# mLSTM keys and queries of 1024 tokens from seven block products of sums in place of eight; key turns moved by threes behind gate units

## The reference, cut to what matters

```
p = h @ w_in                       # h: 2176 x 1024; q, k, v, o, g of 8 heads x 128, and 32 gates
for each head:                     # forward and backward direction
    states C, n from k * wk and v, chunk by chunk
    num = (q k^T * w) v + w0 * q C ;  den likewise ;  hm = num / den
y = ((hf + hb) * sigmoid(o) * silu(g)) @ w_out
x = x + gate * y ; final RMSNorm
```

## Time and profile before

| | |
|---|---|
| time, median of 3 runs | 2608.09 us (2607.71 to 2608.79) |
| span of the profiled execution | 2606.4 us, for which the page gives no time but this |
| busy share of the span | PE 98%, PEld 86%, DVE 49%, ACT 36%, POOL 25% |
| mLSTM heads | seven periods of 150.0 us, and the last head, which ends near 2414 us |
| DMA | 223.84 MB, mean 86 GB/s |

### The profile page before, as it was taken

One profiled execution on the slowest core, in us unless ns is written; L12 is line 12 of the kernel. 1 busy time (PEld: TensorE's weight loads), 2 busy tenths in 40 slices (PEclk: granted clock), 3 DMA queues, 4 the chain that ended last, 5 costly groups with the idle time before them and its releaser, 6 DMA issues.

```text
span 2606.4 us, 49797 instructions
## 1 busy us (share of the span) xinstructions
PE 2560.7 (98%) x18551; PEld 2240.6 (86%) x18551; DVE 1267.2 (49%) x3324; ACT 928.3 (36%) x2157; POOL 657.0 (25%) x826
## 2 busy tenths in 40 slices
PE   7999999999999999999999999999999999999998
PEld 4788888888888887887899999999999999999776
DVE  6774656646465566553242333414243342425876
ACT  5463635626354473223122231312222131313333
POOL 1412222131222213431031130403122040403363
PEclk8999999999999999999999999999999999999999
DMA  9802122030221215431131221303132030415653
GB/s 359 264 19 71 54 55 72 18 99 16 65 66 43 71 60 181 138 122 53 29 72 53 40 84 24 104 21 82 41 52 80 29 95 17 87 44 143 228 156 126
DMA packets 190863, 223.84 MB, mean 86 GB/s; under 512 B 27329, under 2 KB 133585, under 8 KB 188705
## 3 DMA queue, kind: packets, MB, share of 16 engines
q1 hardware_dynamic: 184016, 200.13, 27.3%
q10 hardware_dynamic: 6608, 20.55, 2.0%
HBM read 182.47 MB, written 38.17 MB: 85 GB/s over the span
## 4 chain that ended last, share of the span: by engine, by line
PE 54%; DVE 3%; POOL 2%; issue 1%; DMA 1%; SPq 0%; DVEq 0%; POOLq 0%; ACT 0%
PE psum L590 12%; PE psum L592 12%; PE psum L591 12%; PE psum L2918 2%; PE psum L1643 2%; PE psum L1645 2%; PE psum L1644 2%; PE psum L2985 2%; PE psum L2988 2%; PE psum L2966 1%; PE psum L2909 1%; PE psum L2873 1%; DMA tw<-in_mlstm_w_out 1%; PE psum L1671 1%; PE psum L2996 0%
## 5 line engine op out<-in xcount | busy, mean ns | idle before, releaser
L590 PE MATMUL psum<-h_hi,m_w_lo 128*128 128x384 f32 (+1 forms) x1600 | 594.6, 372 | 0.0
L592 PE MATMUL psum<-h_hi,m_w_hi 128*128 128x384 f32 (+1 forms) x1600 | 574.2, 359 | 0.0
L591 PE MATMUL psum<-h_lo,m_w_hi 128*128 128x384 f32 (+1 forms) x1600 | 573.6, 358 | 0.0
L592 PEld LDWEIGHTS psum<-h_hi,m_w_hi 128*128 128x128 f32 x1600 | 300.9, 188 | 26.9
L590 PEld LDWEIGHTS psum<-h_hi,m_w_lo 128*128 128x128 f32 x1600 | 301.8, 189 | 24.5 <-issue 1.8
L591 PEld LDWEIGHTS psum<-h_lo,m_w_hi 128*128 128x128 f32 x1600 | 302.1, 189 | 22.3
L590 PE MATMUL psum<-h_hi,attn_w_lo 128*128 128x384 f32 (+2 forms) x816 | 297.3, 364 | 0.8 <-DVE attn_w_lo L574 0.8
L592 PE MATMUL psum<-h_hi,attn_w_hi 128*128 128x384 f32 (+2 forms) x816 | 288.9, 354 | 0.0
L591 PE MATMUL psum<-h_lo,attn_w_hi 128*128 128x384 f32 (+2 forms) x816 | 288.8, 354 | 0.0
L1078 DVE CUSTOM_DVE_ANT_0 arena<-psum,wmask,stats 128x640 f32<-128x640 f32 (+2 forms) x256 | 206.0, 839 | 75.0 <-PE psum L1299 74.4
L992 ACT ACTIVATE arena<-arena,stats 128x640 f32<-128x640 f32 (+2 forms) x272 | 213.5, 786 | 70.9 <-DVE stats L1078 69.8
(11 more groups left out here) (415 smaller groups left out, 4736.6 us busy)
## 6 DMA issues: line engine op xcount, KB each, us to landing
m_bc<-gate_rows_mlstm SPq DMA_DIRECT2D x124, 256.0 KB, 3.5
m_w_raw<-in_mlstm_w_in SPq DMA_DIRECT2D x40, 512.0 KB, 4.7
h_full<-gated_output SPq DMA_DIRECT2D x26, 512.0 KB, 4.4
gated_output<-gT SPq DMA_DIRECT2D x8, 1088.0 KB, 5.2
layer_output<-xb_out ACTq DMA_DIRECT2D x17, 512.0 KB, 2.6
h_hi_full<-layer_output SPq DMA_DIRECT2D x17, 512.0 KB, 5.0
out<-h_hi_full ACTq DMA_DIRECT2D x17, 512.0 KB, 5.3
attn_w_raw<-in_attn_w_in SPq DMA_DIRECT2D x16, 512.0 KB, 6.5
```

Source lines behind the costliest of these rows:

```text
L590: pe.matmul(out, self.lo[:, k, :], E.h_hi[:, k, tok], start=(k == 0), stop=False)
L591: pe.matmul(out, self.hi[:, k, :], E.h_lo[:, k, tok], start=False, stop=False)
L592: ins = pe.matmul(out, self.hi[:, k, :], E.h_hi[:, k, tok], start=False, stop=(k == KT - 1))
```

## The change

For heads 1 to 7 the keys and queries of the first 1024 tokens are taken as one product of 2x2 blocks: weights (queries, keys) times (halves of the contraction), tokens (halves of the contraction) times (tokens 0 to 511, 512 to 1023). Seven products of sums replace eight. Each product is four slices of three matmuls of 512 columns.

- Sums of weights (s1 to s4) are formed on GpSimd per head and split by GpSimd and VectorE; the q weights have a buffer of their own (`q_raw`, `q_hi`, `q_lo`), so a head has four loads through `J` in place of five.
- Sums of tokens (T1 to T4), split, are formed once, in four rounds (`token_sums(k)`), two before the gate chain and two behind the q weights of head 0, stored to DRAM (`sums_dram`, 16 tiles of 512 KB) and streamed into a ring of four slots in each head, 16 loads.
- Units k2, q2, k3, q3, k4, q4 of the rest of the tokens stand between the products; VectorE adds the products up in `kT` and `qT`.
- Key turns go by threes into one bank, behind units i = 0 to 5 of o and g (`gate_unit`), products behind i = 1 to 6; the backward sum goes from i = 9 of fifteen to i = 6 of ten. Head 0 keeps its q units, with no key work behind them.
- SP stores the final states at c = 5, after rows 0 to 4, where they stood before all rows.

The hunks in order: the rounds on GpSimd and where they stand, where VectorE's part of them stands, VectorE's loop over the gate units, TensorE's `gate_unit` and `pair` (whose waits are left out), and SP's loop over the rows.

```diff
+def token_sums(k):
+    for t in (T3, T2):
+        pool.wait_ge(s_t[t], at(16 * k))
...
+    pool.tensor_tensor(t_sum(T3), h_hi_of(k + 4, 1), h_hi_of(k, 1), ALU.subtract).then_inc(s_sum, 1)
...
+    pool.tensor_tensor(t_sum(T3), t_sum(T3), h_lo_of(k + 4, 1), ALU.add).then_inc(s_sum, 1)
...
+    pool.tensor_tensor(t_sum(T3), t_sum(T3), h_lo_of(k, 1), ALU.subtract).then_inc(s_sum, 1)
...
+    pool.tensor_tensor(t_sum(T2), t_sum(T3), h_hi_of(k, 0), ALU.add).then_inc(s_sum, 1)
...
+    pool.tensor_tensor(t_sum(T2), t_sum(T2), h_lo_of(k, 0), ALU.add).then_inc(s_sum, 1)
...
+pool.wait_ge(O.s_nat, NG)
...
+token_sums(0)
+token_sums(1)
 J.pool_hi(pool, 1, 2)
+J.pool_hi(pool, 2, 3)
+token_sums(2)
+token_sums(3)
...
 dve.wait_ge(O.s_st[1], 16 * (NS // 2))
+token_sums(0)
+token_sums(1)
 L.dve(dve, O.s_consts, O.s_m0, J)
...
+J.dve_lo(dve, 2)
+token_sums(2)
+token_sums(3)
...
+    for i in range(NP):
+        g = i % NG
+        if 3 * i < NT:
+            dve.wait_ge(s_kT, at(h * NT + min(3 * i + 3, NT)))
+        for s in range(3 * i, min(3 * i + 3, NT)):
+            dve.wait_ge(s_kv, at(h * NT + max(s - 2, 0)))
...
+            dve.tensor_tensor(kw[s % 3][:, :, :], keys, weights_of, ALU.mult).then_inc(s_kw, 1)
+        for c in range(max(3 * i - 3, 0), min(3 * i, NS - 1)):
+            forward(c)
+        if g == NG - 1 and not (last and i >= NG):
+            J.dve_lo(dve, n_o + 1 + i // NG)
...
+    def gate_unit(i):
...
+        J.pe_unit(pe, n_o + i // NG, i % NG, E.bank[(2 + i) % 4])
...
+        for c in range(3 * i - 3, 3 * i):
+            key_products(c)
+        for s in range(3 * i, 3 * i + 3):
+            key_turn(s)
...
+    def pair():
...
+        product(first_bank, a11, 0, early, True)
+        value_turn(h, NG - 1, value_bank(NG - 1))
...
+        J.pe_slices(pe, n_k, 2, E.bank[2], 0, KT)
...
+        product(first_bank, a12, 4, early, False)
...
+        product(second_bank, s2, None, T2, True)
...
+        rest_of_q(2)
...
+        J.pe_slices(pe, n_k, 3, E.bank[2], 0, KT)
...
+        product(second_bank, s3, None, T3, False)
...
+        rest_of_q(3)
...
+        J.pe_slices(pe, n_k, 4, E.bank[2], 0, KT)
...
+        product(first_bank, s1, None, T1, True)
...
+        rest_of_q(4)
...
+        product(first_bank, s4, 4, late, False)
+        product(second_bank, a22, None, T4, False)
...
     for c in range(NT):
...
+        if c == NB - 1:
+            sp.wait_ge(s_kv, at(h * NT + NT))
+        if c == NB:
...
+                sp.wait_ge(s_kvb, at(h * NT + NT))
...
+                for d in range(2):
+                    sp.dma_start(E.new_C[0, 0, d, ds(h, 1)].rearrange("a d e -> d (a e)"), cout[:, d, 0:MHD]).then_inc(s_cst, 16)
+                    sp.dma_start(E.new_n[0, 0, d, ds(h, 1)].rearrange("a d -> d a"), cout[:, d, MHD:E1]).then_inc(s_cst, 16)
...
         if not last and c == NB:
-            load(h * 5 + 5, "v", h + 1)
+            load(weights_no(h, 5), "v", h + 1)
```

More of the change, by code:

```diff
@@ L86, in all_heads, with heads_apart @@
     body(n - 1, True)
+def heads_apart(eng, n, body):
+    body(0, True, False)
+    with eng.Fori(1, n - 1) as h:
+        body(h, False, False)
+    body(n - 1, False, True)
 def at(n):
@@ L546, in sp_load, with pool_hi @@
             sp.dma_start(self.raw[:, :, c0:c0 + w], src).then_inc(self.s_raw, 16)
-    def pool_hi(self, pool, n, loads):
+    def pool_hi(self, pool, n, loads, done=None, halves=(0, 1)):
         pool.wait_ge(self.s_raw, at(loads * 16))
-        for half in range(2):
+        for half in halves:
             if half == 0:
@@ L2566, in head @@
                             sp.dma_start(CC[:, d, slot, MHD:E1], E.a["state_n"][0, 0, d, ds(h, 1)].rearrange("a d -> d a")).then_inc(s_st, 16)
[L2567 to L2574, removed]
+                    n_o, n_g = weights_no(h, 3), weights_no(h, 4)
@@ new lines, in head @@
+                    if first:
+                        load(n_o, "o", h)
+                        store_sums(sp, 2)
+                        store_sums(sp, 3)
+                        for t in range(4):
+                            sp.wait_ge(s_t[t], at(64))
+                    else:
+                        sp.wait_ge(s_sum, at(h * 4 + SUMS))
+                        load(n_o, "o", h)
+                        next_sum(T3)
+                        next_sum(T1)
+                        next_sum(T4)
+                        sp.wait_ge(s_pr, at(h * 7))
@@ L2611, in head @@
                         F.sp_blocks(sp)
-                    if not last:
-                        load(h * 5 + 7, "q", h + 1)
-                all_heads(sp, MH, head)
+                heads_apart(sp, MH, head)
                 sp.wait_ge(s_ogst, at(16 * MH))
@@ L2649, in head @@
                     if not last:
-                        J.pool_hi(pool, h * 5 + 5, h * 5 + 6)
+                        J.pool_hi(pool, n_o + 2, n_o + 3, done + NG)
                     for c in range(NB - 1, NT):
                         rows(c)
[L2653 to L2656, removed]
+                heads_apart(pool, MH, head)
+                pool.wait_ge(J.s_unit, at(UNITS))
                 F.pool(pool)
@@ L2794, in head, with forward @@
                     EARLY_S = 2 if last else 0
-                    for i in range(NA):
-                        u = NG + i
-                        m, g = u // NG, u % NG
-                        if g == NG - 1 and not (last and m == 3):
-                            J.dve_lo(dve, h * 5 + 2 + m)
-                        if m == 3 and g == NG - 1:
+                    def forward(c):
+                        dve.wait_ge(s_kvb, at(h * NT + c + 1))
+                        dve.wait_ge(s_cf, at(h * (NS - 1) + c))
+                        dve.scalar_tensor_tensor(CC[:, 0, c + 1, :], CC[:, 0, c, :], dech[:, 0, c:c + 1],
+                                                 CC[:, 0, c + 1, :], ALU.mult, ALU.add).then_inc(s_cf, 1)
@@ new lines, in rest_of_q @@
+                    def rest_of_q(g):
+                        tok, w = span(g)
+                        for k in range(KT):
+                            pe.matmul(E.bank[3][:, 0:w], q_lo[:, k, :], E.h_hi[:, k, tok], start=(k == 0), stop=False)
+                            pe.matmul(E.bank[3][:, 0:w], q_hi[:, k, :], E.h_lo[:, k, tok], start=False, stop=False)
+                            ins = pe.matmul(E.bank[3][:, 0:w], q_hi[:, k, :], E.h_hi[:, k, tok], start=False, stop=(k == KT - 1))
+                        ins.then_inc(J.s_unit, 1)
```

415 lines of the change are left out of this document (315 added, 100 removed).

## The result

The changed kernel takes 2710.3 us (median of four, 2708.4 to 2710.8); the kernel before, timed beside it, 2608.1. The ratio is 1.039, with a 95% interval of 1.0377 to 1.0403: slower, as forecast, but by 102 us where the sum gave 48, and above the range's end of 2680.

A forecast was written before the change was run, and what follows sets the result against it. TensorE's work plus its waits was taken to bound each head. Terms -19.3 - 2.1 + 24.8 + 28.0 + 11.9 + 1.4 + 3.7 = +48.4 us gave 2656.5 us; range 2624 to 2680.

The forecast's parts named there:

- seventh product and fewer switches: Heads 1 to 7, seven products for eight: -19.3 us; key work by threes, fewer switches in eight heads: -2.1.
- g low half, eight heads: At gate_unit(5), TensorE waits 3.1 us a head for VectorE's low half, behind three weighted keys and state steps: +24.8 us.
- v load, seven heads: At the first step, v weights land late behind the final states' stores: about 4.0 us a head, +28.0.
- token sums, before k and before o: Head 0, four rounds of 14.0 us on GpSimd and VectorE delay k by 7.5 and o by 4.4: +11.9 us.
- head ends: At each head's end GpSimd does two more tensor_tensor beside VectorE before casting k: 0.2 x 7 = +1.4 us.
- last head: Late final stores stand ahead of 4 MB of output weights, delaying row 7 and the last ten steps: about +3.7 us.
- The first part: mLSTM heads: 150.0 us each, TensorE's work plus its waits, at a granted clock of 1.00.
- rival 6: Token sums in head 0: GpSimd contended at its slow rate, +31.6 in place of +11.9, 2676 us; chance 0.05.
- Rivals 2 and 4: Rival 2: v load in time, 2624.8 us, chance 0.13. Rival 4: weights' low parts ready at every first use, 2600, 0.10.
- Rival 7: Seventh product saves nothing, its matmuls spaced wider on streamed operands: +19.3, 2676 us; chance 0.02.
- rival 5: Streamed sums late too, one us for each of three groups in seven heads: +21, 2677.5 us; chance 0.12.

The follow-up runs named there:

- the last trace: All the study's edits together, plus the second round of token sums begun on GpSimd before the key weights' cast, against the changed kernel: 2592.1 us, the fastest of all.
- with the rows held: Changed kernel with SP loading a head's rows only when the g weights' low half is written, VectorE's order unchanged: 2684.2 us.
- the run of all edits together: Changed kernel with g low half first, v load before final stores, token sums moved, last head's output weights before row 4, final stores after row 6: 2597.6 us.

## Why the prediction was right in direction and wrong in size

Measured in the changed kernel's trace, by the prediction's own terms (a wait counts its idle time and the 0.16 to 0.17 us by which the row before it runs past the point where the next matmul would have started):

| term | forecast | measured |
|---|---|---|
| seventh product and fewer switches | -21.4 | about -17.5 |
| g low half, eight heads | +24.8 | +38.0 |
| v load, seven heads | +28.0 | +23.0 |
| token sums, before k and before o | +11.9 | +19.6 |
| head ends | +1.4 | no wait seen |
| last head | +3.7 | +4.2 |
| lower clock behind the waits | none | +34.1 |
| after the last head | none | +1.6 |
| sum | +48.4 | +103.0, of 101.8 in the spans |

The last head's wait is 5.6 us, of which the kernel before had 1.4. The 34.1 are the 32.5 behind the 17 waits and some 1.6 behind the last head's.

**The step that failed: the clock.** The first part took the granted clock of 1.00 as given and priced each wait by the time TensorE stands. It was 1.00 in heads where the engine never stood over 0.3 us. Behind each of the 17 waits the clock falls toward the lower level of 1.2 GHz (0.55 in the third window), for 1.3 to 2.9 us of lost time. Two runs show it apart from all else: with the wait filled by matmuls the stretch vanishes and the clock stays at 1.00, and the old kernel with waits of 2.1 us shows it too. This term, 34.1 us, is the largest part of the 53 missing; the prediction put it at nothing. The spacing in these stretches, 0.427 us for 512 columns, agrees with the 426.7 ns that the Trainium skill (TensorE: Matmul & The Clock Gate, Part 1) gives for 1.2 GHz.

**The g low half.** Mechanism, place and count were right, and with GpSimd idle so was the size, 3.00 against 3.1. The term was mis-sized because VectorE's durations were taken from rows where GpSimd did nothing. The change puts the subtraction beside GpSimd's row products, where state steps take 0.78 and not 0.37, the half 1.17 and not 0.69: 1.7 us a head. The forecast saw this contention for the token sums (rival 6) and at the head ends, not here, and rival 6 priced GpSimd's loss, not VectorE's.

**The v load.** Right in mechanism, and near in size: the store went out 11.1 us before the steps (forecast 11.3), and the weights landed 13.0 after it (forecast 14.5). SyncE's and GpSimd's timelines in head 1:

```profile
1521.44 0.38 SPq L2652 DMA_DIRECT2D out<-m_cout  x1
...
1523.14 0.41 SPq L554 DMA_DIRECT2D m_w_raw<-in_mlstm_w_in  x1
...
1534.60 1.17 POOL L566 CAST m_w_hi<-m_w_raw 128x512 fp32r<-128x512 f32 x2 [30.23 <-DMA m_w_raw<-in_mlstm_w_in]
```

The load landed 1.9 us into the steps and not 3.2, but from there to TensorE's start it took 2.0 us and not 1.3, because VectorE's half took 1.1 beside GpSimd; beyond the 0.26 us of the kernel before, the wait came to 3.3 a head, for 4.0. The estimate of 3.2 us for this load, which the prediction gives beside the sum, did not hold: the load took 11.3 us behind the stores, and still 5.0 ahead of them. (The figure that it is worked out from is one for transfers that GpSimd issues; SyncE issues this one.) Rivals 2 and 4 fell.

**The token sums.** Two places, as forecast, but 11.5 and 8.1 us for 7.5 and 4.4. Some 1 us of the 11.5 is the lower clock again, in the narrow matmuls between the two first rows of TensorE below. GpSimd and TensorE in head 0:

```profile
1211.45 1.30 POOL L2715 TENSOR_TENSOR m_t_stage_raw<-h_hi 128x512 f32<-128x512 f32 x1 [13.66 <-ACT gt_nat L1562]
...
1226.74 1.29 POOL L2715 TENSOR_TENSOR m_t_stage_raw<-h_hi 128x512 f32<-128x512 f32 x1 [3.57 <-DMA token_sums<-m_t_stage]
...
1303.17 0.72 POOL L2786 COPY m_hc<-m_gate_columns 128x102 f32<-128x102 f32 x1
1303.85 0.66 POOL L2787 COPY m_dech<-m_decay_factors 128x32 f32<-128x32 f32 x1
1304.46 1.63 POOL L566 CAST m_w_hi<-m_w_raw 128x512 fp32r<-128x512 f32 x2
...
1244.70 0.58 PE L1897 MATMUL psum<-ident,gt_R 128*1 128x128 f32 x2 [9.04 <-DVE gt_R L1833]
...
1246.84 0.77 PE L598 MATMUL psum<-h_hi,m_w_lo 128*128 128x512 f32 x1 [0.27 <-DVE m_w_lo L582]
...
1306.77 0.77 PE L598 MATMUL psum<-h_hi,m_w_lo 128*128 128x512 f32 x1 [7.95 <-DVE m_w_lo L582]
```

A round is 15.3 us, not 14.0: the casts that run beside VectorE take 1.0 to 1.1, not 0.61. It started 1.1 later, and two copies of 1.4 us, in the code ahead of the o weights' cast, were left out of the walk. The rates of GpSimd's tensor_tensor were the fast ones, so rival 6's price fell.

**The last head.** The wait is 5.6 us, for row 7 behind 4 MB of output weights, as said; with the weights ahead of row 4 and the stores behind row 6 it is gone, and the 1.4 us of the kernel before with it. Against like, the term is 4.2 for 3.7.

**The seventh product.** It saves 2.5 us a head, not 3.0. A product with its switch takes 2.79 us (12 matmuls, 1411.19 to 1413.98 in the last trace) and a remaining unit 4.18, where 2.75 and 4.15 were taken; the sum left out these switches. Rival 7 fell, and rival 5 as well: no product waited.

What stays open: why the slow stretch costs about 1.6 us in some heads and 2.6 in others behind waits of the same length (the low clock lasted longer, 0.55 on the mean over the 6.1 us behind the wait in head 1 against 0.72 in head 3, both behind 4.7 us; what decides it is not shown), and why one head of seven still shows a wait of 0.4 to 1.7 us at its first step with the v load in front. After the last head 1 to 2 us were lost in every version with the change. In the changed kernel the trace shows part of it: a wait of 1.87 us for `h_lo`, at 2556.47, with a clock of 0.57 over the 4 us from 2557. Why that wait arose was not taken apart.

## What to carry to other kernels

Where one engine fills its time, price a new wait by more than its idle time (here 1.4 times over all, 1.8 times for waits of 2.1 us): look up its granted clock behind any wait that the trace already has, and where there is none, count a fall behind each wait of 2 us or more (here most had one, at 1.3 to 2.9 us, and a few had none). When work is moved, read its duration from rows where the same neighbours are busy, and read all that stands between the old place and the new one, copies and switches too. In this kernel the stores in 4-byte pieces belong behind the load that TensorE waits for; two edits of order here were worth 90 us, more than the arithmetic that the change saves.

## What the runs showed of the hardware

Three things were not expected. An idle time of 2.1 us was enough for a fall of the clock in seven of eight heads (0.60 over the 4 us behind it), while waits of 2.4 to 2.8 us at another place passed without one in three of seven heads, and with the rows held waits of 3.00 us before gate_unit(5) in two of eight. After the last head a wait of 1.84 us had a fall behind it in the fastest run (0.66 over the next 5 us) and none in the run of all edits together (1.00). The length of the wait alone does not decide it. Work that is thrown away keeps the clock up: 20 useless matmuls made the kernel 23 us faster. And beside GpSimd's tensor_tensor of 128x256, VectorE's state step of 128x129 took 0.78 us, not 0.37, and its subtraction of 128x512 1.17, not 0.69; GpSimd hardly lost beside the first (0.77 for 0.72), and lost as much beside the second (1.17 for 0.72).
